# Routing by one head, a v ring of six and a fourth weight slot in a gathered expert layer

## The reference, cut to what matters

```python
def peer_ffn(h, w_q, sub1, sub2, u, v):          # 8 heads, 128 sub-keys, the best 16
    qry = (h @ w_q).reshape(B, S, 8, 256)
    s1 = einsum('bshd,hkd->bshk', qry[..., :128], sub1)
    s2 = einsum('bshd,hkd->bshk', qry[..., 128:], sub2)
    v1, i1 = top_k(s1, 16);  v2, i2 = top_k(s2, 16)
    cand     = v1[..., :, None] + v2[..., None, :]           # 16 x 16 pair sums
    cand_idx = i1[..., :, None] * 128 + i2[..., None, :]
    top_s, pos = top_k(cand, 16)
    expert = take_along_axis(cand_idx, pos);  gate = softmax(top_s)
    # per token, over 8 x 16 = 128 slots:
    a = einsum('cd,ced->ce', x_c, u[expert])
    return einsum('ce,ced->cd', gelu(a) * gate, v[expert])
```

## Time and profile before

| | us |
|---|---|
| median of three runs | 2534.91 |
| the runs | 2528.87 to 2535.63 |
| profiled execution, its own time | 2538.69 |
| its span, first to last instruction | 2537.0 |
| PE busy | 2075.4 (82%) |
| DVE busy | 1039.1 (41%) |
| POOL busy | 680.2 (27%) |
| ACT busy | 427.3 (17%) |
| first gather issued at | 232.77 |
| last gather issued at | 1043.43 |
| next block's first weight DMA | 1053.70 |

### The profile page before, as it was taken

The page is one execution under the profiler, slowest core; times in us unless marked ns, Lnnn a source line. Parts: engine busy times, 40 slices in busy tenths (PEclk is TensorE's granted clock), DMA queues, the critical chain, the costliest instruction groups (busy, mean ns, idle before and its releaser), DMA issues. The chain is left out here.

```text
span 2537.0 us, 33649 instructions
## 1 busy us (share of the span) xinstructions
PE 2075.4 (82%) x13344; PEld 1192.8 (47%) x13344; DVE 1039.1 (41%) x2443; ACT 427.3 (17%) x1007; POOL 680.2 (27%) x692
## 2 busy tenths in 40 slices
PE   7997666666766676799797999898798979999987
PEld 6855222222232221278685554444377855544443
DVE  4544665655656645344744111111267441111112
ACT  4321101101101010132331000000035310000000
POOL 2021767767566667302000000000011000000000
PEclk9998787777887886699898999999998989999999
DMA  6315999999899889951354999999933449999996
GB/s 223 111 46 209 345 390 349 368 372 358 335 356 389 322 309 378 328 190 56 119 181 186 428 427 426 428 428 427 393 141 129 179 189 427 427 427 428 428 425 267
DMA packets 166633, 782.76 MB, mean 309 GB/s; under 512 B 18228, under 2 KB 29111, under 8 KB 132279
## 3 DMA queue, kind: packets, MB, share of 16 engines
q1 hardware_dynamic: 89696, 506.60, 49.3%
q0 software_dynamic: 73728, 268.47, 28.3%
q10 hardware_dynamic: 3046, 5.45, 0.7%
HBM read 775.22 MB, written 5.24 MB: 308 GB/s over the span
## 5 line engine op out<-in xcount | busy, mean ns | idle before, releaser
L1582 PE MATMUL banks<-v_rows,row_gates 64*64 64x512 f32 x2048 | 353.0, 785 | 274.1 <-DMA v_rows<-in_peer_v_rows,row_index 165.1
L1556 DVE SCALAR_TENSOR_TENSOR u_rows<-u_rows,h_rows 128x1024 f32<-128x1024 f32 x256 | 313.9, 1226 | 337.0 <-DMA u_rows<-in_peer_u_rows,row_index 325.1
L488 PE MATMUL banks<-weight_ring,window_rows_T 128*64 128x256 f32 x2752 | 312.4, 381 | 36.4 <-DMA weight_ring<-in_moe_w_up 28.3
L1529 POOL DMA_INDIRECT v_rows<-in_peer_v_rows,row_index x256 | 287.6, 1123 | 176.2 <-PE banks L1582 99.5
L1582 PEld LDWEIGHTS banks<-v_rows,row_gates 64*64 64x64 f32 x2048 | 71.3, 157 | 512.2 <-DMA v_rows<-in_peer_v_rows,row_index 410.6
L1529 POOL DMA_INDIRECT u_rows<-in_peer_u_rows,row_index x256 | 264.7, 1034 | 164.0 <-DVE row_index L1675 80.8
L3302 DVE COPY expert_hidden_T<-banks 128x256 f32<-128x256 f32 x64 | 27.2, 425 | 668.0 <-PE banks L3056 668.0
L488 PEld LDWEIGHTS banks<-weight_ring,window_rows_T 128*64 128x64 f32 x2752 | 204.0, 137 | 157.6 <-DMA weight_ring<-in_moe_w_up 39.2
L3201 POOL COPY window_rows_T<-sorted_rows_T 128x512 f32 x64 | 39.9, 624 | 842.5 <-PE banks L488 771.9
L1564 ACT ACTIVATE row_dots_squashed<-row_dots 128x1 f32<-128x1 f32 x256 | 51.0, 202 | 641.5 <-DVE u_rows L1556 418.0
L962 POOL TENSOR_SCALAR inverse_sums<-identity,row_sum 128x128 f32<-128x128 f32 x80 | 47.3, 605 | 385.9 <-DVE row_sum L932 385.1
(11 more groups left out here) (472 smaller groups left out, 2889.8 us busy)
## 6 DMA issues: line engine op xcount, KB each, us to landing
weight_ring<-in_moe_w_gate SPq DMA_DIRECT2D x44, 2048.0 KB, 35.2
weight_ring<-in_moe_w_up SPq DMA_DIRECT2D x42, 2048.0 KB, 38.7
weight_ring<-in_moe_w_down SPq DMA_DIRECT2D x24, 2048.0 KB, 38.5
more_weight_slots<-in_moe_w_up SPq DMA_DIRECT2D x20, 2048.0 KB, 37.5
more_weight_slots<-in_moe_w_down SPq DMA_DIRECT2D x20, 2048.0 KB, 36.4
gain_bias_h_T<-in_moe_w_gate SPq DMA_DIRECT2D x20, 2048.0 KB, 37.6
sixth_weight_slot<-in_moe_w_down SPq DMA_DIRECT2D x20, 2048.0 KB, 37.6
weight_ring<-in_xa_wkv SPq DMA_DIRECT2D x8, 2048.0 KB
```

What stands on the lines that cost most here:

```text
L488: return k.nc.tensor.matmul(out, lhsT, rhs, start=start, stop=stop)
L1529: pool.indirect_dma_start(self.rows[which][:, b, :], None, k.dram[("peer_u_rows", "peer_v_rows")[which]], bass.IndirectOffsetOnAxis(ap=sel ...
L1556: k.nc.vector.scalar_tensor_tensor(u, u, 1.0, self.h[:, self.place(j)[0], :], ALU.mult, ALU.mult, accum_out=self.dots[:, b:b + 1]).then_in ...
L1582: last = k.nc.tensor.matmul(k.ps[places, 2 * tt + half, :], self.gate[tokens, b, :], self.rows[1][tokens, b, half * 512:(half + 1) * 512], ...
```

## The change

Six edits, all in this stage.

1. Routing and gathering go by groups of one head of one tile of tokens: `GROUP_SLOTS` = 16, 16 groups. `route` works on lists of one head, each step followed by its own wait; `top16` calls `between()` after its second and fourth step, so a route has 7 of them, followed by 3 steps and `normalise`.
2. Queries and scores go head by head: two feature units and one score unit for both token tiles. It is 24 units as before. `EARLY` = 6, `EVERY` = 5: 42 units stand ahead of the adds of j = 5, 10, ..., 210.
3. `AHEAD` = 1: a step is dot j + 1, then weigh j.
4. v rows have six buffers, u rows four as before. Gates, dots and gelus keep four.
5. The order of gathers: u and v of 0 to 3, v 4, v 5, u 4, and then for j from 6: u row j - 1, v row j. v now reaches a group first, so it waits for `rows_indexed` too.
6. A fourth weight slot for the stage (`more_slots`).

```diff
 ROW_BUFFERS = 4
-PAIR_SLOTS = 2 * TOPK
+BUFFERS_OF = (4, 6)
+GROUP_SLOTS = TOPK
...
-    for step in steps:
-        for n, item in enumerate(lists):
+    for n, step in enumerate(steps):
+        for item in lists:
             step(*item).then_inc(k.dve_step.up(), 1)
-            if n % 4 == 3 or len(lists) < 4 and n == len(lists) - 1:
-                between()
+        if n % 2:
+            between()
         v.wait_ge(k.dve_step.sem, k.dve_step.count)
...
-    AHEAD = 2
+    AHEAD = 1
...
     def gather_v(self, pool, j):
         k = self.k
         if j < self.COUNT:
-            if j >= ROW_BUFFERS:
-                pool.wait_ge(k.v_rows_used.sem, k.v_rows_used.at(j - ROW_BUFFERS + 1))
+            if j % GROUP_SLOTS == 0:
+                pool.wait_ge(k.rows_indexed.sem, k.rows_indexed.at(j // GROUP_SLOTS + 1))
+            if j >= BUFFERS_OF[1]:
+                pool.wait_ge(k.v_rows_used.sem, k.v_rows_used.at(j - BUFFERS_OF[1] + 1))
             self.gather(pool, 1, j)
...
+        k.stream.more_slots(sb("one_more_first_slot", [P, 1, SLOT], ctx=c))
         units = []
-        for p in range(PH // 2):
-            for m in range(4):
...
+        for h in range(PH):
+            for side in range(2):
+                units.append(feature_products(k, hT, DC, tiles["w_peer_q"] + h // 2, 512, (2 * (h % 2) + side) * P, P,
+                                              [(qT[:, h % 2, side, :], 0, P)], "a"))
+            prods = [lambda ps, h=h, tt=tt, side=side:
+                     mm(k, ps[:, (2 * tt + side) * PK:(2 * tt + side + 1) * PK],
+                        qT[:, h % 2, side, tt * P:(tt + 1) * P], sub[:, side, h, :])
+                     for tt in range(NT) for side in range(2)]
+            units.append((None, prods, "a", [copy_out(k, sc[:, h, :, :, :].rearrange("p t s n -> p (t s n)"), P, 512)]))
...
+            h, tt, of = slots(group)
+            dve.wait_ge(k.act_evacuated.sem, k.act_evacuated.at(3 * h + 3))
+            top16(k, [(sc[:, h, tt, s, :], spare[:, s, 0:PK], best[:, s, :], place[:, s, :]) for s in range(2)], between)
...
             for s in range(2):
...
+                hot = spare[:, s, :].rearrange("p (j a) -> p j a", a=TOPK)
+                k.v(v.tensor_tensor(hot, digitf[:, s, :].unsqueeze(2).to_broadcast(hots),
+                                    iota[:, :].unsqueeze(1).to_broadcast(hots), ALU.is_equal))
+                k.v(v.tensor_tensor(hot, hot, placef[:, s, :].unsqueeze(1).to_broadcast(hots), ALU.mult))
+                k.v(v.tensor_reduce(rows[:, tt, s, of], hot, AX, ALU.add))
                 between()
...
-    EARLY, EVERY = 12, 6
-    groups = g.COUNT // PAIR_SLOTS
+    EARLY, EVERY = 6, 5
+    groups = g.COUNT // GROUP_SLOTS
...
-            for j in range(ROW_BUFFERS):
+            for j in range(4):
                 g.gather_u(pool, j)
                 g.gather_v(pool, j)
-            for j in range(ROW_BUFFERS, ROW_BUFFERS + g.AHEAD):
-                g.gather_u(pool, j)
-            for j in range(ROW_BUFFERS, g.COUNT):
-                g.gather_u(pool, j + g.AHEAD)
+            for j in range(4, 6):
+                g.gather_v(pool, j)
+            g.gather_u(pool, 4)
+            for j in range(6, g.COUNT + 1):
+                g.gather_u(pool, j - 1)
                 g.gather_v(pool, j)
...
-                route(dve, group, lambda: step(group * PAIR_SLOTS))
+                route(dve, group, lambda: step(group * GROUP_SLOTS))
                 routed[done + g.AHEAD] = group
-                for _ in range(4):
-                    step(group * PAIR_SLOTS)
+                for _ in range(3):
+                    step(group * GROUP_SLOTS)
                 normalise(dve, group)
```

## The result

The changed kernel takes 2519.18 us (median of seven runs, 2514.67 to 2524.71), the kernel before in the same series 2534.5 us (seven runs, 2528.87 to 2536.34). The ratio is 0.9948, interval 0.9933 to 0.9962: 15.3 us between the medians, 13 by the ratio. The forecast was 2497, a gain of 37.8. The sign held, and so did the wide range (2470 to 2536); the forecast's own range, 2482 to 2516, and the size did not.

What follows compares the result with a forecast made beforehand. POOL's instruction stream was taken as the bottleneck. Terms -13.8 - 2 - 20 - 6 + 4 = -37.8 us from the profiled 2538.69 gave 2500.9, hence 2497 for the median; own range 2482 to 2516, wide range 2470 to 2536.

Steps and rivals of the forecast that it cites:

- The bound: Gathering stage: POOL's instruction stream is the bottleneck, 706 of 811 us; the DMA is busy but not at its best.
- Part 1: Before the first gather: routing one head needs only two feature units, so gathers start at 219.0 us, -13.8 us.
- rival e: Start of the stage: gathers do not start earlier (memory_2_T or a late sub-key), losing 6 to 14 us; 2507, chance 0.08.
- Part 2: First gathers of the loop: six v buffers give POOL three more gathers to issue; -2 us, between 0 and -5.
- Part 3, nine places: Steady gather loop: v's release stays nine gathers on in POOL's order, so two extra buffers change nothing; single units still stall.
- Part 3, pairing: Token units in the loop: pitch five with six buffers spares every second unit its wait; 39.8 us halves, -20 us.
- Feature and score units: Shorter units ahead of adds in the loop: waits fall from 24 to 18 us despite six more units, -6 us.
- Part 4: Routing on DVE in the loop: 15 one-head routes replace 7 two-head ones; +4 us, between 0 and +15.
- (b): Units in the loop: no pairing occurs, each stalls POOL as before; -5.8 us, 2529, chance 0.20.
- (c): Units in the loop: the buffers cover the units' waits wholly; -76 us, 2459, chance 0.08.
- (d): POOL's gathers: more start just inside a dot, each stretched by 0.9 us; slower, 2551 with 60 more, chance 0.12.

Runs made afterwards that it cites:

- second pair: The kernel before and the changed kernel, unedited, profiled again on another chip: changed kernel 2505.57 us, ratio 0.995; kernel before 2525.14 us in its single run.
- 13 places: Changed kernel with six v buffers kept but old gather order and dots two ahead: 2463.99 us, 0.979; kernel before with only six v buffers: 2464.72 us, 0.9786.
- first pair: The kernel before and the changed kernel as first measured and profiled: 2534.5 and 2519.18 us, ratio 0.9948.
- eleven: Changed kernel with only the gather order edited, u row j then v row j, dots still one slot ahead: 2470.39 us, 0.9789.
- half dots: Changed kernel with old gather order and dots two ahead, each dot over only 512 of its 1024 columns, gathers whole: 2436.59 us, 0.9657.

## Why the prediction was right in sign and wrong in size

**The bound: right for these two kernels.** Each variant moved the time by what it did to POOL's stream, and the DMA had room: 359 GB/s at a share of 0.96 in the kernel before, up to 403 when POOL was let go. There the engines' share is 1.02; the prediction did not name them as the next limit.

**Part 1, the first gather: right.** Forecast -13.8, measured -14.9 in the stage and -12.6 in absolute time. Routing one head took 10.06 us for 9.5, and started 2.39 us after the copy for 2.4. No wait for memory_2_T; the slot was worth nothing (rival e is out).

**Part 2, filling: right in kind, smaller.** Forecast -2. The first 40 us show +2.6, but 3.4 of that is the unit ahead of add 5; without it -0.8, and in the second pair too (4.6 to 7.4, with 3.6 for that unit). The stall of 3.40 us in the earlier trace rows became several shorter ones, the longest 2.42 before u row 8. The extra v buffers let POOL issue v rows, but the u row behind them waits for a dot just the same.

**Part 3, nine places: right, and read too weakly.** Both series (7, 9, 11, 13 places; four buffers with the old order equal to six with the new) show that the edit's own halves cancel. The prediction said this in a sentence and went on to credit the six buffers with the pairing. What it should have asked is what the buffers give when they are not spent: 56 us.

**Part 3, pairing: the effect was right, its reason half false and its size too large.** Three of the four second token units are spared, in the first stretch at 14.38 and 20.75 us apart for the forecast 14 and 18. The reason given, that the pitch is five and the buffers are six, fell with the run that has four: with a pitch of five it pairs all the same, with six it doesn't even with six buffers. What does hold of the reason is that the second unit's last add needs no row that is issued later than the one POOL was held at. That the spared units ran at the full granted clock, 7.13 us for 9.1, was no part of the forecast and helped it. The term: -20 was forecast, -14.1 measured (-9.2 in the second pair of profiles). It was mis-sized in that four waits were reckoned at 5.0 us, and there were five, up to 6.44 in the first pair and 6.75 in the second. Feature and score units: -6 forecast; 21.8 to 22.8 measured, with the unit ahead of add 5, so +1.0 (31.7 to 27.8 in the second pair). 24 us were put to them before and there were 21.8, and the six units moved into the loop took the gain back, one of them 3.4 us alone.

**The term left out: u gathers behind dots, +8.6** (2.0 to 10.6, and 1.8 to 10.7 in the second pair). This is the step that failed most. The prediction costed the v gathers' wait and put the u side at nothing: it never asked what a later u gather does there, and took one landing of 5.2 us for all, where some came at up to 16, with 11 us of room. The row stood in the view of waits of the kernel before, 7.1 us in five waits, and the earlier trace rows is one of them. At the same nine places the kernel with four v buffers and the old order has 2.2 us of it and the changed one 10.7, so the six v buffers, the order and the dots one slot ahead make it between them; no run gives each its part. With more places it grows as v rows hold POOL back less.

**Part 4: not shown.** +4 was forecast for steps that slip behind routing. No view of these kernels isolates that; the gathers' own time rose by 3.6 us in the first pair and 1.7 in the second, which is another mechanism, and the nearness of the two numbers is luck. DVE's busy time between the first gather and the last add rose by 35 us (475.5 to 510.3) for the forecast 18; its idle time before dots fell from 337.0 to 294.6 us, and POOL never waited for `row_index` in the loop.

**The sum of the loop.** +3.6 own time, -0.8 filling, +8.6 u gathers, -14.1 token units, +1.0 feature and score units, -0.5 other v, -2.5 unexplained: -4.7, measured -4.4. With the start -17.0 to the last issue, -15.7 to the last add, 15.9 in the span, 15.3 between the medians. Missing to the forecast are 9 us of u gathers, 7 of features, 6 of tokens, and 1 each of filling, of the start and after the last issue; the unexplained pauses gave 3 back.

**The rivals.** (b), pairing absent, would have given 2529 and is nearer to the measured 2519 than the forecast is, but its mechanism is not there: most of the units do pair. (c), the buffers covering the units, is what happens with 13 places and for the most part with eleven (token units 12 us; -35 us against the changed kernel), and I gave it 0.08 with the right objection, the nine places. (d), gathers stretched by dots, did not change with the edit (1.08 to 1.086), but the half dots show the mechanism to be worth 53 us of POOL's own time.

## What to carry to other kernels

Before a buffer is added to a ring, count the places in the issuing queue from the last transfer that the release depends on to the transfer that needs the release. A change of order and a change of the look-ahead can spend new buffers exactly, and then the ring is deeper and nothing is hidden. When one wait is bought off, look up the second row of the view of waits of that engine: its buffer is what is late next (here the u rows behind the dots), and it belongs in the sum. And look at the DMA engines' busy share, not only at their rate: at 0.96 deeper rings were worth 83 us here, and once it was 1.02 half of what POOL gained elsewhere was lost again.

## What the hardware showed that I had not expected

On the first chip POOL made pauses of up to 2 us beyond the ordinary one, most with the buffer free for 2 to 5 us, before v gathers, in both kernels: the eight of the row "remote" are among them, one is this of the changed kernel.

```profile
490.21 1.09 POOL L1532 DMA_INDIRECT v_rows<-in_peer_v_rows,row_index  x1 [1.67 <-remote]
```

They sum to 27.7 and 25.2 us there and to 0 to 6 in all later runs, with the same two kernels at 1.6 and 2.4. Without them the span of the kernel before is 13.6 us shorter, not 26: POOL then stands before the same adds a little longer. What causes them stays open, and with one chip that shows them, chip and time cannot be told apart.

A gather's 0.94 us can double when it starts inside a dot: 1.84 in the earlier trace rows, up to 1.99 for a gather that starts with the dot. With 0.94 and 0.30 us each, 512 gathers of 512 KB would need some 636 us of POOL; no kernel here came below 718. The two that came near, at 721.6 and 718.0, have the DMA engines at a share of 1.02, so that floor is not POOL's alone.
